# Score columns of attention sinks by one bfloat16 product of three pieces

## The reference, cut to what matters

```python
sink_l = jnp.broadcast_to(sink.astype(jnp.float32).reshape(1, N_KV_A, GQA_GROUP, 1, 1),
                          (B, N_KV_A, GQA_GROUP, BLOCK, 1))
...
s_loc = jnp.where(ok, s_loc, NEG_INF)
s_ctx = jnp.einsum('bqkgd,bckd->bkgqc', qi, kc).astype(jnp.float32)
p = jax.nn.softmax(jnp.concatenate([s_ctx, s_loc, sink_l], axis=-1), axis=-1).astype(v.dtype)
```

## Time and profile before

| | |
|---|---|
| Time, median of 3 runs (range) | 1921.88 us (1921.09 to 1924.34) |
| Span of the profiled execution | 1922.9 us |
| Busy: TensorE products, its loads | 1777.8 us (92%), 924.5 us (48%) |
| Busy: VectorE, ScalarE, GpSimd | 783.6, 370.0, 230.7 us |
| Chain of work that ended last, by engine | PE 74%, DMA 16%, DVE 4%, ACT 3% |
| DMA traffic | 525.69 MB, mean 273 GB/s |

### The profile page before, as it was taken

One profiled execution on the slowest core, in us unless ns is written; L12 is line 12 of the kernel. 1 busy time (PEld: TensorE's weight loads), 2 busy tenths in 40 slices (PEclk: granted clock), 3 DMA queues, 4 the chain that ended last, 5 costly groups with the idle time before them and its releaser, 6 DMA issues.

```text
span 1922.9 us, 31130 instructions
## 1 busy us (share of the span) xinstructions
PE 1777.8 (92%) x13332; PEld 924.5 (48%) x13332; DVE 783.6 (41%) x1623; ACT 370.0 (19%) x806; POOL 230.7 (12%) x315
## 2 busy tenths in 40 slices
PE   6999999999799999999999999999949999888896
PEld 3886567854344444444443876567423333222222
DVE  2995665647621111111111674665242333323233
ACT  3213455622200000000001313556120000000001
POOL 1001330001011211112111101420000000000000
PEclk8999998999799999999999999999979999999999
DMA  9543000076779999999997843000869999999996
GB/s 387 219 154 153 1 1 1 2 295 228 270 294 389 400 394 395 392 395 393 391 392 316 314 172 132 1 23 2 327 230 346 402 410 403 405 412 404 412 414 265
DMA packets 83074, 525.69 MB, mean 273 GB/s; under 512 B 11280, under 2 KB 13600, under 8 KB 24064
## 3 DMA queue, kind: packets, MB, share of 16 engines
q1 hardware_dynamic: 66096, 476.70, 61.8%
q0 software_dynamic: 14640, 46.81, 7.9%
q10 hardware_dynamic: 2208, 0.26, 0.1%
HBM read 506.94 MB, written 16.79 MB: 272 GB/s over the span
## 4 chain that ended last, share of the span: by engine, by line
PE 74%; DMA 16%; DVE 4%; ACT 3%; issue 1%; SPq 0%; POOL 0%; DVEq 0%; ACTq 0%; POOLq 0%
PE psum L1511 16%; PE psum L1505 9%; PE psum L1514 8%; PE psum L1223 6%; DMA ring<-in_w_up 6%; PE psum L1187 6%; DMA arena<-in_w_up 6%; PE psum L1396 6%; PE psum L1299 5%; PE psum L1346 3%; PE psum L1317 3%; PE psum L1273 2%; PE psum L1595 2%; ACT arena L1032 2%; PE psum L1257 1%
## 5 line engine op out<-in xcount | busy, mean ns | idle before, releaser
L1511 PE MATMUL psum<-ring,arena 128*32 128x512 f32 x1920 | 250.4, 593 | 0.0
L1505 PE MATMUL psum<-ring,arena 128*64 128x512 f32 x888 | 209.0, 605 | 20.1 <-DMA ring<-in_w_down 9.9
L1108 ACT ACTIVATE arena<-psum 128x768 f32<-128x768 f32 (+1 forms) x32 | 22.5, 704 | 903.1 <-PE psum L1514 462.1
L1505 PE MATMUL psum<-arena 128*64 128x512 f32 x648 | 150.8, 600 | 13.9 <-DMA arena<-in_w_down 7.6
L1514 PE MATMUL psum<-ring,arena 128*32 128x256 f32 x1920 | 147.6, 379 | 0.0
L1396 PE MATMUL psum<-ring,arena 128*128 128x512 f32 x320 | 144.7, 603 | 0.0
L1032 ACT ACTIVATE arena<-psum,smx 128x768 f32<-128x768 f32 (+4 forms) x160 | 118.9, 748 | 111.4 <-DVE smx L1858 111.1
L1505 PEld LDWEIGHTS psum<-ring,arena 128*64 128x64 f32 x888 | 58.6, 138 | 153.4 <-issue 110.8
L1858 DVE TENSOR_REDUCE smx<-psum 128x1 f32<-128x768 f32 (+4 forms) x160 | 115.8, 765 | 39.4 <-PE psum L1257 27.3
L1514 PEld LDWEIGHTS psum<-ring,arena 128*32 128x32 f32 x1920 | 62.4, 110 | 143.6 <-issue 143.6
L1511 PE MATMUL psum<-arena 128*32 128x512 f32 x960 | 125.2, 593 | 0.0
(11 more groups left out here) (291 smaller groups left out, 2094.8 us busy)
## 6 DMA issues: line engine op xcount, KB each, us to landing
ring<-in_w_up SPq DMA_DIRECT2D x84, 1024.0 KB, 28.2
ring<-in_w_down SPq DMA_DIRECT2D x81, 1024.0 KB, 28.6
ring<-in_w_gate SPq DMA_DIRECT2D x78, 1024.0 KB, 28.3
arena<-in_w_gate SPq DMA_DIRECT2D x50, 1024.0 KB, 28.9
arena<-in_w_down SPq DMA_DIRECT2D x47, 1024.0 KB, 28.5
arena<-in_w_up SPq DMA_DIRECT2D x44, 1024.0 KB, 27.1
ring<-in_w_adat SPq DMA_DIRECT2D x32, 1024.0 KB, 6.8
ring<-in_w_in SPq DMA_DIRECT2D x18, 1024.0 KB, 19.1
```

The source lines that it names most:

```text
L1505: ins = mm(psum[64 * n:64 * n + 64, b * 512:(b + 1) * 512], lhs(k), w[:, n * 512:(n + 1) * 512], start=k == 0, stop=k == KD - 1)
L1511: ins = mm(psum[r0:r0 + 32, b * 512:(b + 1) * 512], lhs(k)[:, 32 * g:32 * g + 32], w[:, n * 512:(n + 1) * 512], start=k == 0, stop=k == KD ...
```

## The change

The sink's column is no longer made by a float32 product with the identity. At the start VectorE copies the 16 sinks to `sink_rest`, a free place in `arena`. The 16 float32 columns of `small` are then seen as 32 bfloat16 columns, `sinkp`: the last 16 are set to 1, the first 16 to 0. Then, three times, the rest is rounded to bfloat16, written into one row of the first 16 columns (row 0, 32, 64), and subtracted from the rest (not after the third). Three bfloat16 pieces hold a float32 number exactly. In a W step a single bfloat16 product has one column of ones, repeated 128 times (step 0), as stationary operand and the sink's bfloat16 column as the moving one: it sums the three pieces over the rows, in float32, into each of the 128 partitions.

```diff
-    sinkb = small[:, 158:SMALL].rearrange("p (l h) -> p l h", l=DEPTH)
+    sinkb = small[:, 158:SMALL]
+    sinkp = sinkb.bitcast(BF16)
+    sink_rest = arena[:, LAMBDAS:LAMBDAS + 16]
+    sink_piece = arena[:, LAMBDAS + 16:LAMBDAS + 24].bitcast(BF16)
...
                     h = 2 * st.n + x
-                    mm(psum[:, s0 + st.keys:s0 + st.keys + 1], ident[:], sinkb[:, l, h:h + 1], start=True, stop=True
-                       ).then_inc(L["S"], 1)
+                    mm(psum[:, s0 + st.keys:s0 + st.keys + 1], sinkp[:, 16:17].broadcast_to([P, P]),
+                       sinkp[:, HW * l + h:HW * l + h + 1], start=True, stop=True).then_inc(L["S"], 1)
...
         dve.wait_ge(s_cload, 16)
+        dlink(dve, dve.tensor_copy(sink_rest, sinkb))
+        dve.memset(sinkp[:, 16:32], 1.0)
+        dlink(dve, dve.memset(sinkp[:, 0:16], 0.0))
+        for row in (0, 32, 64):
+            dlink(dve, dve.tensor_copy(sink_piece, sink_rest))
+            dve.tensor_copy(sinkp[row:row + 1, 0:16], sink_piece[row:row + 1, :])
+            if row < 64:
+                dlink(dve, tt(sink_rest, sink_rest, sink_piece, ALU.subtract))
         for l in range(DEPTH):
             ts(sublc[:, l:l + 1], pack[:, 60 + l:61 + l], 1.0 - lam_init(l), None, ALU.mult)
```

## The result

| | before | changed |
|---|---|---|
| Median (range) of the paired runs | 1921.49 us (1918.81 to 1924.34) | 1906.49 us (1904.81 to 1910.79) |
| Ratio, 95% interval | | 0.9922 (0.9903 to 0.9941) |
| Span of the profiled execution | 1922.9 us | 1904.8 us |
| TensorE products, busy | 1777.8 us | 1756.9 us |

The direction was right, the size was not.

A forecast was written before the change was run, and what follows sets the result against it. TensorE was held busiest, with windowed steps bound in turn by TensorE, the sink-to-exponentials chain and the values-product chain. Savings 1.7 + 2.8 + 1.1 + 2.0 = 7.6 us took 1921.9 to 1914.3 us; range 1910 to 1920.5.

The forecast's parts named there:

- The sum: Savings over the 40 windowed attention steps of both layers: 1.7 + 2.8 + 1.1 + 2.0 = 7.6 us.
- That time saved in attention moves everything after it: Expert loads wait for attention's last values product, so everything later moves forward with its end, one for one.
- Price of the new product: Bfloat16 sink product in windowed steps: between 0.05 us, like a mask product, and 0.11 us; 0.05 taken.
- d: Time saved per sink product in windowed steps: 0.14 us, with 0.08 and 0.16 as ends.
- The rival with 0.11: New product costs near 0.11 us, like a float32 pass; 4.6 us saved, 1917.3; chance 0.24 with the 0.15 case.
- the price that I gave to one whose load is hidden by nothing: New product costs 0.15 us; 2.5 us saved, 1919.4; chance 0.24 together with the 0.11 case.
- The nine intervals capped at 0.22 us: Windowed steps like that of 338.31 us, where VectorE and ScalarE allow some 0.22 us each: 2.0 us.
- four intervals that I held for filled: Windowed steps where the chain from the values product already fills the interval; they save nothing.
- the two half-clock intervals: Two TensorE-led windowed steps from 301 to 311 us, saving 2 x 0.28 us each: 1.1 us.
- a rival in which the stretch goes: Half-clock stretches go, some 3 us more saved: 1911; chance 0.08.
- The forecast of 4.7 and 7.6 us for the two loads: First expert load issued about 4.7 us earlier in layer 0, about 7.6 in layer 1.
- The prologue at nothing: Eleven added VectorE instructions at the start, 2.2 us, covered by the load of w_ada; uncovered 2 to 4 us.

The follow-up runs named there:

- f32_ones: Kernel before with one float32 column of 1/128, repeated 128 times, in place of the identity as stationary operand: 1924.05 us, ratio 1.0005.
- no_sink: Kernel before with the sink's column left out, no product for it and the softmax over the keys alone: 1907.46 us, ratio 0.9933.
- bf16_six: Changed kernel with each bfloat16 sink product made six times in a row, the last one signalling: 1917.26 us, ratio 0.998.
- a_gapfill: Changed kernel with 50 unread 128-column bfloat16 products ahead of the third block's transposes in layer 0's output projection: 1909.63 us, ratio 0.9938.
- b_gapfill2: Kernel before with 50 unread 128-column bfloat16 products ahead of the third block's transposes in layer 0's output projection: 1918.33 us, ratio 0.9988.
- b_gapfill: Kernel before with 56 unread 128-column bfloat16 products in layer 0's output projection, one block too late, behind the gap: 1924.79 us, ratio 1.0021.
- a_pad128: Changed kernel with 128 unread one-column bfloat16 products near the start: 1907.7 us, ratio 0.9932.
- b_pad128: Kernel before with 128 unread one-column bfloat16 products near the start: 1922.03 us, ratio 1.0001.
- b_again: Kernel before, unaltered, measured once more: 1922.3 us, ratio 0.9999.
- f32_three: Kernel before with each float32 sink product made three times, the last one signalling: 1951.81 us, ratio 1.016.

## Why the prediction was right and wrong

- **In short.** The sum had 7.6 us. The cheaper product gave 8.8 with the half clock equal, 1.2 more than the sum; less half clock in the W steps gave 2.9, by my estimate; the output projection of layer 0, which the sum and the rivals had at nothing, gave about 4 in the profiles. That stage is the largest part of what was missing.
- **That time saved in attention moves everything after it: right; "one for one": wrong.** From the end of the output projection to the next attention stage the two pairs of profiles agree within 2.4 us, with no sign of the change in it; nothing was taken back. But the first stage after attention, the output projection, gave more of its own.
- **Price of the new product: the wrong end.** I took the mask's spacing, 0.05, as the lower end, arguing that a mask product's own load has to fit in it. It does (0.056 us a product with its load and 128 moving columns), but the argument gives an upper bound for the load, not the price of a product with one column. (The bound used was 0.05; the mask rows are mostly 0.06 apart.) It is 0.03, and 0.025 in a run of six, so d is 0.16, the end of my bounds, where my sum gave 8.3. The rival with 0.11 fell: a pass with a load of 128 columns takes 0.107 us in float32, but six bfloat16 loads and products together take 0.15. Nor does any run show 0.15 us for one such product, the price that I gave to one whose load is hidden by nothing.
- **The nine intervals capped at 0.22 us: mis-sized.** They gave 0.32 (4.59 to 4.27). I had read the chain of the step at 338.31 us as running without the sink's product. But its maxima started 0.54 us behind L1926 (339.55 to 340.09), and 0.47 after the change (336.73 to 337.20): they had waited 0.07 us for the "S" of the very product that shrank. The hand-over to TensorE is 0.05 us, not 0.07. In f32_ones, where the product costs 0.19 us with another stationary operand, it is 0.54 again, and in no_sink 0.46. That is 0.9 us in the sum. One of the four intervals that I held for filled, 3.36 us, also went to 2.95. With these and with d at 0.16 the sum is 9.6 us, or 9.0 with the two half-clock intervals counted at full clock, against the 8.8 measured.
- **The half clock: right kind, too small.** I had 1.1 us for a cheaper product in the stretch and gave 8% to a rival in which the stretch goes, at 3 us more. In the profiles it mostly went, for an estimated 2.9 us. So the W steps gave 11.7 us in all, as against 7.6 in the sum. The forecast of 4.7 and 7.6 us for the two loads was 6.2 and 17.7. From the first windowed scores the first is 7.8 us earlier (the changed profile had started 1.6 us later), and the second has the output projection inside.
- **The output projection: missing from the sum and from the rivals.** Some 4 us came from a stage of which the change touches no line. In the earlier trace rows the DMA is at work there, and the chain of waits of before has a residual store of 16.5 us; I had read neither that chain nor the wait of 3.5 us with the half clock behind it, since I looked only for whether the saving would be given back. The runs show that this stage goes with the place of TensorE's instruction stream, and that filling the gap alone makes the kernel before 2.6 us faster. 11.7 + 4 = 15.7 us, against 15.0 to 16.2 in the medians; since the kernel before won 1.5 us or less in the medians from the better place, the close agreement is in part luck.
- **The prologue at nothing: right.** My estimate was 2.2 us; L1680 moved by 2.05, from 3.20 to 5.25 us, and its cover held.
- **A slip without effect.** Slice 27 of the earlier trace rows has 23 GB/s, not 1 or 2.
- **What stays open.** By which way a fetch's place delays or speeds the landing of the residual is not shown; only that landing and stage follow it. Why the kernel before got 1.5 us or less from the better place, and the changed one 4.7 or more, is in part put down from start and half clock of a few profiles, not tested; nor is it known why the later start on chips 3 and 5 does not show in the medians of the kernel before (1920.8 to 1921.8 us on all four chips). And whether the half clock in W goes because the steps are shorter or because the gaps lie elsewhere was not separated; bf16_six, with steps nearly as long as before's (4.51 us where before has 4.59) and yet 6.8 and 0 us at half clock, speaks against the length alone, in one profile.

## What to carry to other kernels

A float32 product with one column cost two passes with their loads here, 0.19 us; where the value has exact bfloat16 pieces that fit into unused rows of the contraction, one bfloat16 product did it in 0.03 us, a sixth of the time, with a repeated column or an identity as stationary operand. Before capping a gain by "another chain", look whether that chain itself waits for the instruction that shrinks, to a hundredth of a microsecond. And list the waits followed by half clock in all stages, also those not touched: here a change in the number of TensorE's instructions went with 4 us in one of them. An effect of a few microseconds should be measured at two places of the instruction stream, and on the same chip, before it is put down to the edit.

## What the runs showed of the hardware

- One-column bfloat16 products with their own loads of 128 columns follow each other in 0.025 to 0.03 us; products with such a load and 128 moving columns follow each other in 0.056 (the 50 and 56 filler products of a_gapfill, b_gapfill2 and b_gapfill). A one-column float32 pass with such a load takes 0.107; with 128 moving columns a pass takes 0.036, 0.060 or 0.110 to 0.122 where 32, 64 or 128 columns are loaded (L1424, L1346, then L1412 and L1317 of before).
- The place of TensorE's 16 KB instruction fetches relative to a stage full of DMA went with a difference of 4 us in that stage, over 16 profiles, and with the landing of its first store, over 20; 256 instructions more at the start (128 products and their loads) restored both the place and, within 1.6 us, the time of the stage (91.4 us in a_pad128, 96.7 in b_pad128).
- In six profiles of kernels identical up to there (before, b_again, no_sink, f32_three, b_gapfill, b_gapfill2) the first windowed scores came anywhere from 292.0 to 296.8 us, with different stretches at the lower granted clock ahead of them. Over all kernels it went with the chip: 291.9 to 294.6 us on chips 0 and 12, 294.5 to 296.8 on chips 3 and 5.
